# Fetching a mixture-of-experts layer's rows by indirect DMA for all four sets, ranking the sets on their own, and loading weights in a ring of 15 pieces

## The reference, cut to what matters

```python
def hier_moe(h, ...):
    t = h.reshape(-1, shp[-1])
    lg = (t @ w_rg + b_rg)
    oh_g = one_hot(argmax(lg), N_GROUPS)                 # top 1 of 4 groups
    p_sel = sum(softmax(lg) * oh_g, keepdims=True)
    le_sel = einsum('tge,tg->te', t @ w_re + b_re, oh_g)
    top_v, top_i = lax.top_k(le_sel, 2)                  # top 2 of the group's 8 experts
    wk = softmax(top_v) * p_sel
    comb = one_hot(oh_g) x one_hot(top_i) x wk
    for g in range(N_GROUPS):
        a, u = t @ w_g[g], t @ w_u[g]                    # 1024 -> 256 for each of 8 experts
        out = out + einsum(silu(a) * u * comb, w_d[g])   # 256 -> 1024
x = x2 + hier_moe(rmsnorm(x2, g_norm2))
```

## Time and profile before

| what | value |
|---|---|
| median of 3 runs | 697.99 us (697.93 to 699.54) |
| profiled execution, its own time | 699.08 us |
| its span, first to last instruction | 697.3 us |
| TensorE busy, of the span | 656.2 us, 94% |
| VectorE, ScalarE, GpSimd busy | 345.0, 258.7 and 119.1 us |
| granted TensorE clock, mean | 0.979 |
| read from and written to memory | 167.99 and 7.48 MB (decimal) |
| chain that ended last | TensorE 78%, issue 9%, VectorE 5%, DMA 4% |

### The profile page before, as it was taken

One profiled execution on the slowest core, in us unless ns is written; L12 is line 12 of the kernel. 1 busy time (PEld: TensorE's weight loads), 2 busy tenths in 40 slices (PEclk: granted clock), 3 DMA queues, 4 the chain that ended last, 5 costly groups with the idle time before them and its releaser, 6 DMA issues.

```text
span 697.3 us, 9451 instructions
## 1 busy us (share of the span) xinstructions
PE 656.2 (94%) x3512; PEld 433.4 (62%) x3512; DVE 345.0 (49%) x733; ACT 258.7 (37%) x501; POOL 119.1 (17%) x129
## 2 busy tenths in 40 slices
PE   5999999999999999998999999889998998999895
PEld 4887888777887767777777878543443433343331
DVE  4748349974465555554356742764251433333211
ACT  5673433344324445555844341532111312211100
POOL 0019336651002001000000200013003001202100
PEclk9999999999999999999999999899998999899998
DMA  8956432444116433104875599289999999999980
GB/s 320 394 229 216 141 125 91 165 161 157 62 62 209 162 122 121 63 31 159 311 255 228 162 355 413 85 331 357 420 422 421 420 420 422 420 421 420 421 358 24
DMA packets 34048, 175.61 MB, mean 252 GB/s; under 512 B 4256, under 2 KB 4400, under 8 KB 20816
## 3 DMA queue, kind: packets, MB, share of 16 engines
q1 hardware_dynamic: 30896, 163.29, 60.0%
q0 software_dynamic: 3104, 11.68, 4.7%
HBM read 167.99 MB, written 7.48 MB: 252 GB/s over the span
## 4 chain that ended last, share of the span: by engine, by line
PE 78%; issue 9%; DVE 5%; DMA 4%; ACT 2%; SPq 1%; POOL 1%; DVEq 0%; ACTq 0%; POOLq 0%
PE banks L1874 14%; PE banks L1538 13%; PE banks L1540 13%; PE banks L1539 13%; PE banks L1898 8%; DMA wgu<-in_wexp 4%; PE banks L1862 2%; PE banks L1726 1%; PE banks L1811 1%; PE banks L1909 1%; PE banks L1699 1%; PE banks L1740 1%; SPq L755 1%; PE banks L1700 1%; PE banks L1718 1%
## 5 line engine op out<-in xcount | busy, mean ns | idle before, releaser
L1139 DVE TENSOR_TENSOR w_lo<-raw,w_hi 128x1024 fp32r<-128x1024 f32 (+1 forms) x81 | 128.2, 1595 | 88.0 <-ACT w_hi L902 87.8
L1538 PE MATMUL banks<-w_hi,hT_hi 128*128 128x512 f32 x312 | 124.0, 397 | 1.5 <-ACT z L929 0.8
L1874 PE MATMUL banks<-wgu,xs 128*64 128x512 f32 x512 | 118.2, 600 | 3.7 <-DMA wgu<-in_wexp 3.7
L1539 PE MATMUL banks<-w_lo,hT_hi 128*128 128x512 f32 x312 | 121.6, 390 | 0.0
L1540 PE MATMUL banks<-w_hi,hT_lo 128*128 128x512 f32 x312 | 121.6, 390 | 0.0
L902 ACT ACTIVATE w_hi<-raw 128x1024 fp32r<-128x1024 f32 x79 | 83.4, 1056 | 88.7 <-PE banks L1540 84.5
L1874 PEld LDWEIGHTS banks<-wgu,xs 128*64 128x64 f32 x512 | 39.2, 138 | 79.5 <-issue 72.1
L1538 PEld LDWEIGHTS banks<-w_hi,hT_hi 128*128 128x128 f32 x312 | 58.6, 188 | 15.3 <-issue 2.0
L1540 PEld LDWEIGHTS banks<-w_hi,hT_lo 128*128 128x128 f32 x312 | 58.6, 188 | 12.5
L1539 PEld LDWEIGHTS banks<-w_lo,hT_hi 128*128 128x128 f32 x312 | 58.6, 188 | 11.3
L1898 PE MATMUL banks<-wdn,act_T 128*64 128x512 f32 x256 | 61.9, 627 | 1.0
(11 more groups left out here) (336 smaller groups left out, 981.2 us busy)
## 6 DMA issues: line engine op xcount, KB each, us to landing
wgu<-in_wexp SPq DMA_DIRECT2D x64, 1024.0 KB, 20.4
raw<-in_wstream SPq DMA_DIRECT2D x79, 512.0 KB, 4.4
wdn<-in_wexp SPq DMA_DIRECT2D x32, 1024.0 KB, 19.5
foxc<-in_foxc POOLq DMA_DIRECT2D x8, 512.0 KB, 4.7
memv<-in_memc SPq DMA_DIRECT2D x8, 512.0 KB, 4.8
memk<-in_memc SPq DMA_DIRECT2D x8, 512.0 KB, 4.8
xT<-in_xT SPq DMA_DIRECT2D x1, 1536.0 KB, 11.2
xtok<-in_xtok SPq DMA_DIRECT2D x1, 1536.0 KB, 7.8
```

The lines of the kernel that those rows point to most:

```text
L1139: dve.tensor_tensor(w_lo[:, i % PART_SLOTS, cols], raw[:, i % RAW_SLOTS, cols], w_hi[:, i % PART_SLOTS, cols].bitcast(F32), ALU.subtract). ...
L1538: mm(out, xh, wh, start=start, stop=False, skip_group_check=True)
L1539: mm(out, xh, wl, start=False, stop=False, skip_group_check=True)
L1874: ins = mm(ps[64 * e2:64 * e2 + 64, 2 + a % 2, :], xs[:, (a // 2) % 2, k, c0:c0 + CAP], wgu[e % EXP_SLOTS][:, 512 * k:512 * k + 512], star ...
```

## The change

- `x_parts` and `compact` go. Set 0 takes the way of the other sets: rows are fetched from `y` by `rows_in` and split by `split_rows`.
- `route` is cut in pieces. `route_group` finds the group, ranks the four groups alone (`token_ranks` with 4 columns) and gives the tokens' rows (`info` 0). `route_best` 0 and 1 find the experts, `route_slots` ranks them (32 columns, `info` 1), `route_weights` and `info` 2 follow behind the first half of the first `gu`.
- `y` is stored by GpSimd (`store`, semaphore `s_fk_out`), and the first fetch waits for both halves.
- Weights lie in a ring of 15 pieces of 1 MB in the order of use: for each pair gate/up first halves of both experts, second halves, down. Twelve pieces are issued where `load_first` was; 12 to 14 lie over `w_hi` and `w_lo` and wait for the last granule; each later one waits for the piece 15 before it. `xs` moves over the raw slots.
- `gu` is cut in two steps, `gu` and `gu_rest`, 16 matmuls each. `rows_in` of set g+1 moves from the first pair of set g to the second, `split_rows` to the third. The code for a full set's overflow is adapted (left out below).

```diff
@@ schedule
-    s += [("residual", 1), ("squares2", 1), ("turn_x2", 1), ("norm2",), ("logits", 1), ("x_parts",), ("route",)]
+    s += [("residual", 1), ("squares2", 1), ("turn_x2", 1), ("norm2",), ("logits", 1), ("route",)]
@@ moe_schedule
     plain("pick_group", 0)
-    plain("weights", 0)
-    step("compact", 0, 0, 3)
+    plain("best", 0, 0)
     plain("info", 0)
+    plain("rows_in", 0)
+    plain("best", 0, 1)
+    plain("slots", 0)
+    plain("info", 1)
     plain("pick", 0)
-    s.append(("compact_low", 0, 0, 3, None))
-    step("compact", 0, 1, 7)
-    s.append(("compact_low", 0, 1, 7, None))
+    plain("split_rows", 0)
     for j, bank in enumerate((5, 6, 2, 3)):
         step("gather", 0, j, bank)
-    step("rows", 0, 0, 0)
     for p in range(PAIRS):
...
+        step("gu", p, 0, 2 + p % 2)
+        if p == 0:
+            plain("weights", 0)
+            plain("info", 2)
+            step("rows", 0, 0, 7)
         plain("slot_weight", p)
...
-        step("gu", p, 0, 2 + p % 2)
+        plain("gu_rest", p)
         if p:
             plain("y_out", p - 1)
             plain("back", p - 1)
+        if pl == 2 and more:
+            plain("split_rows", g + 1)
         plain("silu", p)
...
             if more:
-                plain("info", g + 1)
-            if g == 0:
-                plain("rows_in", 0)
-            if more:
-                plain("rows_in", g + 1)
+                plain("info", g + 3)
         if pl == 1 and more:
-            plain("split_rows", g + 1)
+            plain("rows_in", g + 1)
@@ SyncE
-            def load_expert(e):
...
+            def load_piece(c):
+                pair, part, e = c // 6, c % 6 // 2, 2 * (c // 6) + c % 2
+                if c >= PIECES:
+                    old = c - PIECES
+                    sp.wait_ge((gu_half, gu_ready, dn_ready)[old % 6 // 2], old // 6 + 1)
+                load(piece[c % PIECES][:, :], io["wexp"][e, :, 2048 * part:2048 * part + 2048], piece_in[c % PIECES])
...
-                    load_first()
-                    sp.wait_ge(x2_ready, T)
-                    sp.dma_start(io["y"][:, :, 0:512], x2[:, :, 0:512]).then_inc(s_x2, 16)
-                elif kind == "residual" and i == 1:
-                    sp.wait_ge(x2_ready, 2 * T)
-                    sp.dma_start(io["y"][:, :, 512:1024], x2[:, :, 512:1024]).then_inc(s_x2, 16)
+                    for c in range(12):
+                        load_piece(c)
...
-            for e in range(4, NG * NE):
-                load_expert(e)
+            sp.wait_ge(gran_used, NGRAN)
+            for c in range(12, 6 * PAIRS):
+                load_piece(c)
@@ GpSimd
+                elif kind == "residual":
+                    pool.wait_ge(x2_ready, T * i + T)
+                    store(io["y"][:, :, 512 * i:512 * i + 512], x2[:, :, 512 * i:512 * i + 512], s_fk_out)
...
                 elif what == "rows_in":
-                    pool.wait_ge(info_out, a + 1)
-                    pool.wait_ge(s_x2, 48)
+                    pool.wait_ge(info_out, a + 3 if a else 1)
+                    pool.wait_ge(s_fk_out, 48)
                     if a >= 2:
                         pool.wait_ge(s_y, 16 * (a - 1))
```

More of the change, by code:

```diff
@@ L430, in program @@
         pT = at("pT", [P, 2, 256], o_work + 21 * KB)
-        o_exp = [o_z + 24 * KB * i for i in range(4)] + [o_raw]
-        wgu = [at(f"wgu{i}", [P, 4096], o_exp[i]) for i in range(EXP_SLOTS)]
-        wdn = [at(f"wdn{i}", [P, 2048], o_exp[i] + 16 * KB) for i in range(EXP_SLOTS)]
+        o_piece = [o_z + 8 * KB * i for i in range(12)] + [o_raw + (16 + 8 * i) * KB for i in range(3)]
+        piece = [at(f"piece{i}", [P, 2048], o_piece[i]) for i in range(PIECES)]
         wgu_o = [at(f"wgu_o{i}", [P, 6144], o_z + 24 * KB * i) for i in range(2)]
@@ L515, in program @@
         gu_half, ot_hi, ot_lo = sem("gu_half"), sem("ot_hi"), sem("ot_lo")
-        wgu_in = [[sem(f"wgu_in{i}_{half}") for i in range(EXP_SLOTS)] for half in range(2)]
-        wdn_in = [sem(f"wdn_in{i}") for i in range(EXP_SLOTS)]
+        piece_in = [sem(f"piece_in{i}") for i in range(PIECES)]
         class Chain:
@@ L1098, in _ @@
             with if_overflow(act):
+                act.wait_ge(acc_done, 2 * NG)
+                for t in range(T):
+                    ins = act.activation(ov_diag[:, t, :], ident, ACT.Copy, scale=rstd2[:, t:t + 1])
+                ins.then_inc(xhi_ready, 1)
                 for k in range(KT):
@@ L1322, in _ @@
                     ins.then_inc(xs_odd, 1)
-                elif what == "gu" and a == 0:
+                elif what == "gu_rest" and a == 0:
                     overflow_weights(dve, chain)
@@ L1802, in _ @@
                         ins.then_inc(lg_ready, 1)
[L1803 to L1814 removed]
+                elif kind == "route":
+                    token_ranks(0, 32, 4, [T * NR + 4 * t for t in range(T)])
             kw = dict(skip_group_check=True)
@@ L1824, in bank_free @@
                     pe.wait_ge(xs_odd if j % 2 else xs_even, 2 * a + j // 2 + 1)
-                elif what == "compact":
-                    pe.wait_ge(xg_lo_ready, 2 * a + j + 1)
                 elif what == "rows":
@@ L1833, in _ @@
                 bank_free(old)
[L1834 to L1849 removed]
+                if what == "info":
+                    pe.wait_ge(info_in, min(a, 2) + 1)
+                    pe.wait_ge(info_out, a)
+                    pe.wait_ge(pick_group, group_of_info(a) + 1)
+                    if a >= 3:
+                        pe.wait_ge(hT_evac, 4 * a - 11)
+                    n0, n1 = (4, 6) if a == 0 else (0, 6)
+                    for t in range(T):
+                        ins = mm(ps[:, 4, 256 + 2 * n0:256 + 2 * n1], pick_g[:, t, :], info_parts[:, t, n0:n1, :].rearrange("p n s -> p (n s)"), start=t == 0, stop=t == 2, **kw)
                     ins.then_inc(info_done, 1)
+                elif what == "slots":
+                    token_ranks(1, 0, 32, [NR * t for t in range(T)])
                 elif what == "rows":
[L1852 removed]
+                    pe.wait_ge(info_out, a + 3)
                     for n in range(4):
@@ L1863, in _ @@
                     ins.then_inc(gather_done, 1)
-                elif what == "gu":
-                    for k in range(KT):
+                elif what in ("gu", "gu_rest"):
+                    half = what == "gu_rest"
+                    for k in range(4 * half, 4 * half + 4):
                         if k % 2 == 0:
```

265 lines of the change are left out of this document (109 added, 156 removed).

## The result

The change takes 692.61 us (median of 6 runs, 691.75 to 694.96); the kernel before, timed with it, 699.57 us (6 runs, 697.93 to 701.39). The ratio is 0.9905, 95% interval 0.9881 to 0.9930: faster by 1.0%. Two more sets of runs of the same kernel gave 0.9909 [0.9893, 0.9924] and 0.9899 [0.9882, 0.9916].

The account below looks back on a forecast made before the run. The weight stream's end, set by 20.4 us of DMA idle time, was taken as the bound. Less idle 3.5, order 2.5 and clock 1.2 took 7.2 off 697.3: span 690.1, median 690.8; range 686 to 697.

Parts of the forecast that it names:

- The end hangs on the stream: Experts' stage: the end depends on when the weight stream ends, hence on 20.4 us of idle DMA time before 480 us.
- The second half of y: Store by GpSimd before the first fetch: ready at 434.6, landing between 442.2 and 449.7, value taken 448.5.
- The routing chain: VectorE's routing before the first expert: `info` at 444.7, `pick` at 450.3, so the saved VectorE time is worth nothing by itself.
- A cold TensorE: First `gather` and `gu` at half clock: `gather` 4.3 us instead of 2.14, first half of `gu` ends at 463.0.
- The idle time of the stream: DMA engines around the routing: 16.9 us idle against 20.4, so the last piece lands 3.5 us sooner, at 676.6.
- the second gap: Weight stream after the first released pieces, first `down` at 473.0 against work to 474.5: about 0.5 us idle at most.
- a second hole before 480: Weight stream after the first hole: another idle stretch before 480 us would show the forecast wrong; no size given.
- The order of the last pieces: Last pair: last gate/up piece lands two pieces before the end, at 671.6; the order gives 2.5 us.
- the moved steps: `rows_in`, `split_rows` and small matmul groups moved: 3.10 us stalls and half speed go, twice, but hidden; matmuls cost 1 us.
- the end terms: Last `down`: 2.5 us sooner by piece order and 1.2 because TensorE reaches the last pair without loss of clock.
- Cold at the last pair: Rival, last pair: a wait before `gu_rest` costs TensorE clock, 2.2 us more, 693.0; chance 0.16.
- The absolute time: Whole kernel: span of 690.1 plus 0.7 gives a median of 690.8 us, 1.0% faster.

Follow-up runs that it names:

- `rows_in` early: The change with `rows_in` of sets 1 to 3 back in the first pair of a set, ahead of the next `back`: 691.59 us, 0.9891 of the kernel before.
- y twice: The change with the second half of y stored twice and the first fetch waiting for both stores: 697.20 us, 0.9979 of the kernel before.
- ring of 12: The change with 12 weight pieces in the ring instead of 15: 698.11 us, 0.9980 of the kernel before.
- first control: The change itself, unedited, timed again beside the kernel before on the same chip: 692.36 us, 0.9909 of that kernel.
- last six by expert: The change with its last six pieces ordered gate/up, gate/up, down of expert 30, then of 31: 698.34 us, 0.9988 of the kernel before.

## Why the prediction was right

It held in direction, size and mechanism: a gain of 7.0 us of span, forecast as 7.2. That the span came within 0.2 us (690.3 for 690.1) is luck: the six executions of the change had spans of 689.8 to 693.1, and the parts below missed by more, in opposite ways. By its steps:

- **The end hangs on the stream.** Right. The stalls of 3 us could be put back at no cost (`rows_in` early), a later first expert cost its full delay (y twice), and with fewer pieces ahead the end followed the hole (ring of 12).
- **The second half of y.** Landing forecast at 448.5, measured 446.2: 2.3 us too late a value, within its two ends. Fetch at 447.1 instead of 448.6: between landing and issue lie 0.9 us, of which the forecast had 0.1. It took 4.2 us (4.5 forecast from the earlier trace rows), rows in at 451.3 instead of 453.1. The two-port lock that the Trainium skill (SBUF — State Buffer, Who interferes with whom) warns of took nothing here: both stores kept GpSimd for 0.75 us, with VectorE busy for most of that time, and the issue of the fetch 1.10; whether VectorE was in such a mode then is in no row. What the store did lose, 11.3 us for 4.1, it lost beside the weights in the other queue, which goes with the account of the Trainium skill of engines that go round between the queues (DMA: Bandwidth & Descriptors, Queues, rings and completion order); the exchange itself is in no row.
- **The routing chain.** `info` came at 444.25 (forecast 444.7), `pick` ended at 450.36 (450.3), both hidden behind y and the fetch, as said.
- **A cold TensorE.** It happened, but cost less: the `gather` took 3.7 us and not 4.3. Half of `gu` ended at 461.1 and not 463.0, mostly because the rows were in 1.8 us sooner; the half itself took 4.2 us, 4.1 forecast.
- **The idle time of the stream.** 17.5 us against 16.9 forecast, so the last piece came 2.9 us sooner and not 3.5, but the parts were missed in opposite ways. From 440 to 470 us it was 14.8 (forecast 16.4 without the second gap), thanks to the earlier y. The second gap was called 0.5 at most and measured 10 x 106/421 = 2.5; "a second hole before 480" was one of the forecast's own signs of being wrong, and it came. Two things would make it: the first released pieces went out 1.9 us sooner and were through sooner, and the first `down` came late. The trace has `act_h` only at 468.01, though its input `act_g` was ready at 466.44: `overflow_weights`, eight instructions from 465.76 on that only prepare for the case of an overflowing set, had moved behind `gu_rest` and stood ahead of it on VectorE. The forecast listed the moved steps and left this one out. TensorE idled 1.40 and 0.77 us there. Moving it behind `act_h` was not tried, so its share of the gap is not shown. (On the page of the kernel before, 420 to 422 GB/s stand in the ten slices from 488 to 662 us, not in twelve; the rate of 421 used in these sums stands.)
- **The order of the last pieces.** Last landing 677.2 (676.6), last gate/up piece about 672.0 (671.6), `down` at 677.64 (677.0), end 690.3 (690.1). The sum of the end terms, 3.7 us (2.5 by order and 1.2 by clock), measured 4.1. The split was wrong, and that its sum was close is luck: the order alone is worth 4.6 us within the change and 1.0 in the kernel before. The two terms are not separate; the order pays only when TensorE is on time. In the kernel before it was not: the `gu` of the last pair began at 674.55 behind the `down` before it, and its last gate/up piece held it up by 0.7 us at most.
- **Cold at the last pair.** Did not come; the wait before the last half was 1.31 us. One of 1.95 us in the third pair from the end did cost clock (5.34 us for 3.65), and the next pair had no wait at all: a late TensorE found its pieces, as the rival's text said of itself. The same wait cost no clock in the first control (1.94 us, then 3.65).
- **The absolute time.** 690.8 forecast, 692.61 measured. The 0.7 us added to a span came from three runs of before; with three more runs beside the change the median of that kernel rose by 1.6 us, and a span here lies 1.8 below its own execution's time.

Not run: the kernel before with its own routing and only a deeper stock of pieces. There `x_hi` and `x_lo` lie where the three extra pieces would go, so the new routing is what makes room for them; that it gives more than room is not shown. With the new routing and the new order but a ring of 12 the ratio is 0.998.

## What to carry to other kernels

When a stage is bound by a stream of loads, count the time in which the queue is empty and the order of the last few loads, and leave stalls of the computing engine in the middle alone: here two stalls of 3 us with their loss of clock were free, and the order of the last six of 96 loads was worth 4.6 us. An extra buffer ahead and an early small fetch share the same DMA engines; here their gains did not add. When steps are reordered, list each instruction that now stands ahead of one that releases a buffer, the bookkeeping ones too.

## What the runs showed of the hardware

- A store of 768 KB by GpSimd took 4.1 us when the stream of weights had just ended, 6.0 when it ended 4.5 us after the issue, 11.2 to 11.4 when it ran on beside it, and 7.3 to 7.8 on SyncE's own queue behind the older pieces. One indirect fetch of 128 rows took 4.2 to 4.4 us with no weights beside it, 5.7 and 7.0 with more of it beside the stream, and 8.5 to 10.0 wholly beside it.
- The same wait can cost clock or not: in the third pair from the end a wait of 1.93 to 1.95 us was followed by 14 matmuls in 5.34 us in two executions of the change, and by 3.65 us in the first control and in the kernels with y stored twice and with the last six by expert.
- The clock of TensorE comes back after different times: in one execution of the changed kernel all 16 matmuls of the `gather` and the start of `gu` ran at 1.2 GHz; in the control, after a wait as long (3.88 us for 3.83), the last three of the 16 ran at full speed already and `gu` took 3.65 us instead of 4.24.
- The clock may fall once between 200 and 250 us, in code that no kernel here changes (mean 0.97 for 1.00 in 3 of 14 profiles); the stores of y then come 1.3 to 1.9 us later.
- With some eleven pieces of 1 MB outstanding (an estimate: 27.3 us from issue to landing, 2.49 us a piece), each issue of a further piece kept SyncE for 2.1 us; the stream itself stayed at 419 to 424 GB/s.
